# Scores of two attention mixers in clusters of four maps, half of them in borrowed accumulators

## Chip, core and metric

The kernel runs on one core of a Trainium2 chip. The metric is the device time of one execution in microseconds, as the median of several.

## What is computed

Two layers of a decoder trunk with four attention mixers, 256 positions, 1024 channels, four heads per mixer. Cut to what matters here:

```python
xn = rms_norm(x)
h = xn @ w_in                      # columns of the four mixers
# B: two softmax maps per head of 32 channels each
p1 = masked_softmax(q1 @ k1.T * scale); p2 = masked_softmax(q2 @ k2.T * scale)
o_b = rms_norm((p1 - lam * p2) @ v)
# C: with 256 positions, plain causal attention, heads of 64 channels
o_c = masked_softmax(q @ k.T * scale) @ v
# A: stick-breaking attention; D: compressed, selected and window branches
merged = sum(sigmoid(xn @ w_gate[i] + b_gate[i]) * (o_i @ w_branch[i]) for i in 0..3)
x = x + merged @ w_out
x = x + (silu(hn @ w_ffn_gate) * (hn @ w_ffn_up)) @ w_ffn_down    # hn = rms_norm(x)
```

## The kernel before

The five kinds of large products (in, gate, branch, out, ffn and down) stream their weights in chunks of 256 rows by 512 columns (the last input group has 396 columns). A chunk is loaded by SP into `w_raw` (four buffers), copied by ScalarE into `w_hi`, and the remainder is formed by VectorE in `w_lo`; ScalarE and VectorE work two chunks ahead. TensorE then does eight products with `w_hi` and four with `w_lo`, 12 for each chunk (L648). A load of chunk n waits until `w_lo` of chunk n-4 is made.

The attention work lies between the chunks. Each small piece of it is a step with a kind and a name, and the table `PLAN` says in which slot u it stands. All engines walk the slots in the same order. In slot u TensorE does the steps first and then the products of chunk u. ScalarE and VectorE do the steps of a `RANK` below 3, then the split of chunk u+2, then the steps of rank 3 and above, in order of rank. The slots 0 to 23 are the input projection, 24 to 55 the gates, 56 on the branch products.

The steps of this case, per layer:

- `sm` computes causal scores of a pair of maps (`scores`, `causal`, L733). Per map there are two matmuls: the second 128 queries against 256 keys (256 columns), the first 128 against 128 (128 columns). In mixer B a map has 32 channels, so a matmul uses 32 rows of the array; in C, D (and A's `z`) it uses 64. The two maps of a pair lie on different rows, and each writes to its own PSUM bank, S0 or S1 (`maps_of`, `banks_of`). B has four pairs, C two, D four. VectorE then reads both banks with four fused operations, mask and row maximum (L1271); ScalarE takes the four exponentials with sums (L963); VectorE normalises (`p`, L1285 to L1304).
- `pt` transposes probabilities on TensorE into bank TP (L772), and ScalarE copies them out (`ptb`, L1038). `pv` multiplies with V (L788 for B, L797 for the others).
- `qk` transposes queries or keys (L720), `cr` and `kct` are small pieces of D's compressed branch (L851, L862), `ck` and `cv` its compression (L810), `cs` its scores (L872).

The order on an engine is thus written out by hand through `PLAN` and `RANK`. PSUM has eight banks: TP, OB, S0 and S1 for attention, and two pairs `acc` for the results of the large products, which alternate from one result to the next (`bank_pair`). A pair is idle from the time when ScalarE (`proj`) or VectorE (`zg` and the others) has read a result until the next but one result starts.

Of the kernel before, what the change touches and what calls it, by code (L numbers as in the profile page):

```python
# [14 lines left out]
P = 128  # L15
# [34 lines left out]
NCH = len(CHUNKS)  # L50
# [21 lines left out]
def in_cols(g):  # L72
# [40 lines left out]
def maps_of(mixer, n):  # L113
# [11 lines left out]
    "x0": 0, "f0": 0, "m0": 0, "proj": 4, "zg": 4.5, "merge": 0.5, "xadd": 0.5, "act": 3.5, "silu": 4, "hid": 4.5, "split": 5, "rows": 1, "Acum": 5.5,  # L125
    "Dp": 6, "cpv": 6, "sig": 4.5, "Cpv": 3, "cbuild": 1.5, "kct": 4.5, "x": 0.5, "Asp": 6, "Bpv": 4.5, "ck": 1,
    "cv": 1.5, "cs": 3.5, "prep": 0.5, "Csm": 3, "Dpv": 4.5, "lambda": 2.5, "stats": 1.5, "subln": 6, "Bsm": 4,
    "Bpt": 6, "ngate": 1.5, "Cp": 5, "kcprep": 2, "f": 4, "Bp": 5.5,
# [3 lines left out]
def steps():  # L132
# [3 lines left out]
    def put(u, *step):  # L136
        at[u].append(step)
# [11 lines left out]
    for mixer in "ABCD":  # L149
        if mixer != "A":  # L150
            put(PLAN["prep"]["BCD".index(mixer)], "prep", mixer)
        for n in range(PAIRS[mixer]):
            for kind in {"A": ("z", "sp", "cum", "pv"), "B": ("sm", "p")}.get(mixer, ("sm", "p", "pv")):
# [89 lines left out]
TP, OB, S0, S1 = range(4)  # L243


def banks_of(step):
    kind, a = step
    if kind == "pair":
        if a[0] == "o":
            return (TP,) if a[1] == 1 else (OB,)  # L250
        return ((TP, S0, S1, OB)[a[1]],)
    if kind in ("qk", "pt", "kct", "cpt", "cr", "cks"):
        return (TP,)
    if kind in ("z", "cum", "sm", "cs"):
# [50 lines left out]
def trunk_kernel(nc, x, x_t, w_in, w_gate, w_branch, w_out, w_ffn, w_ffn_down,  # L305
                 norm_g, gains, lam, cmp_pe, cmp_w, b_gate, const, masks, out):
    with ExitStack() as ctx:
# [206 lines left out]

        block = ctx.enter_context(nc.Block())
# [70 lines left out]
        def _(pe):  # L586
            def bank_free(l, step):

                for b in banks_of(step):
                    prev = previous(l, BANK_USES[b], step)  # L590
                    if prev:

                        before = ("cum", prev[1][1]) if prev[1][0] == "z" else prev[1]
                        ev = read_dve if reader_of(before) == "dve" else read_act
                        pe.wait_ge(ev.sem, ev.at(prev[0], before))

            def products(l, u):
# [125 lines left out]
            def causal(buf, maps, swap=False):  # L723

                for b in (S0, S1) if swap else ():
                    pe.matmul(att[:, b, :].rearrange("p (s c) -> p s c", c=P)[:, 0:3:2, :], ident16,
                              mask_a.unsqueeze(1).to_broadcast([P, 2, P]), start=True, stop=False, skip_group_check=True)
                first, second = ((0, 2 * P), (P, 2 * P)) if swap else ((0, P), (0, 2 * P))
                areas = ((0, first, 0), (1, second, 2 * P)) if swap else ((1, second, P), (0, first, 0))
                for n, (t, (c0, c1), at) in enumerate(areas):  # L730
                    for i, (r, q, k) in enumerate(maps):
                        still, move = (k, q) if swap else (q, k)
                        mm = pe.matmul(att[:, S0 + i, at:at + c1 - c0], qkt[buf][r, still, t * P:(t + 1) * P],  # L733
                                       qkt[buf][r, move, c0:c1], start=not swap and n == 0, stop=n == 1,
                                       skip_group_check=True)
                return mm

            def scores(l, step):
                kind, a = step
                bank_free(l, step)  # L740
                mixer, n = ("A", a) if kind == "z" else a
                if n == 0:
# [3 lines left out]
                buf, maps = maps_of(mixer, n)  # L746
                mm = causal(buf, maps, swap=mixer == "A")
                mm.then_inc(att_done.now(step), 1)
# [372 lines left out]
        def _(dve):  # L1121
# [36 lines left out]
            def do(l, step):  # L1158
# [103 lines left out]
                elif kind == "sm":  # L1262
# [306 lines left out]
```

## Time and profile before

| | us |
|---|---|
| median of 3 executions | 859.01 (858.69 to 859.31) |
| the profiled execution | 859.28 |
| its span, first to last instruction | 857.5 |
| TensorE busy | 851.2 (99%) |
| VectorE busy | 598.6 (70%) |
| ScalarE busy | 500.4 (58%) |
| GpSimd busy | 267.7 (31%) |
| HBM traffic | 154.45 MB, 180 GB/s |

Durations of single instructions come from the one profiled execution. A row of the timeline gives the start of a group, the time from there to the end of its last instruction, and how many there were; matmul ends are modelled, so the distance from the start of one group to the start of the next is the time that TensorE spent on it. An fp32 matmul of the attention steps is recorded twice (x8 for four matmuls), since it runs in two passes. The two layers show the same pattern, the second some 424 us after the first.

### The profile page before, as it was taken

The page shows a single profiled execution, that of the slowest core. Times are in us where ns is not written, and L with a number is a line of the kernel's source. Part 1 is how long each engine was busy: PE and PEld are TensorE (multiplying, and loading weights), DVE is VectorE, ACT ScalarE, POOL GpSimd, SP SyncE. Part 2 cuts the span into 40 slices and gives each one's busy share as a digit, 9 for nine tenths or more (in the row PEclk, how much of TensorE's full clock was granted, in tenths as well). Part 3 has the DMA queues.
Part 4 walks back from the last instruction along what each step waited for, and adds up shares of the span by engine and source line. Part 5 has one row for each costly group of instructions (what it writes and reads, how often), then busy time and mean ns, then how long its engine had stood idle before and what let it go on. Part 6 is the DMA issues. An engine that isn't in the chain of part 4 may idle for free.

```text
span 857.5 us, 12229 instructions
## 1 busy us (share of the span) xinstructions
PE 851.2 (99%) x4530; PEld 706.0 (82%) x4530; DVE 598.6 (70%) x932; ACT 500.4 (58%) x837; POOL 267.7 (31%) x253
## 2 busy tenths in 40 slices
PE   9999999999999999999999999999999999999998
PEld 6888887787888888888888788878788888888886
DVE  5566868558868888864555668676587698888552
ACT  6785645676457555553457775556654665556431
POOL 0087714003304444420000967230042144444100
PEclk9999999999999999999999999999999999999999
DMA  9756454445656555565565455454445565565652
GB/s 333 248 156 199 153 189 144 149 146 173 195 170 199 192 183 191 179 206 177 172 212 192 136 194 179 167 172 148 143 159 193 169 213 186 184 188 189 201 193 73
DMA packets 68443, 155.24 MB, mean 181 GB/s; under 512 B 5409, under 2 KB 7841, under 8 KB 68129
## 3 DMA queue, kind: packets, MB, share of 16 engines
q1 hardware_dynamic: 68096, 154.20, 55.4%
q8 instruction: 36, 0.59, 0.3%
q10 hardware_dynamic: 288, 0.27, 0.1%
q14 instruction: 23, 0.18, 0.1%
HBM read 153.40 MB, written 1.05 MB: 180 GB/s over the span
## 4 chain that ended last, share of the span: by engine, by line
PE 96%; DMA 1%; DVE 1%; ACT 1%; issue 0%; SPq 0%; ACTq 0%
PE acc L648 60%; PE acc L637 18%; PE acc L642 9%; PE att L733 2%; PE att L797 1%; PE att L772 1%; PE att L695 1%; PE att L720 1%; DMA w_raw<-in_w_in 1%; PE att L788 1%; PE att L756 0%; DVE xs L1204 0%; DVE w_lo L1135 0%; ACT sq_dump L1010 0%; PE att L810 0%
## 5 line engine op out<-in xcount | busy, mean ns | idle before, releaser
L1135 DVE TENSOR_TENSOR w_lo<-w_raw,w_hi 128x1024 fp32r<-128x1024 f32 (+1 forms) x276 | 357.7, 1307 | 121.4 <-ACT w_hi L905 119.3
L905 ACT ACTIVATE w_hi<-w_raw 128x1024 fp32r<-128x1024 f32 (+1 forms) x275 | 286.5, 1051 | 98.0 <-PE acc L648 69.1
L648 PE MATMUL acc<-w_hi,xt 128*128 128x512 f32 (+1 forms) x1024 | 261.8, 397 | 0.2 <-ACT xt L928 0.2
L648 PEld LDWEIGHTS acc<-w_hi,xt 128*128 128x128 f32 x1024 | 185.5, 188 | 38.9 <-issue 2.2
L637 PE MATMUL acc<-xt,w_hi 128*128 128x512 f32 x704 | 176.8, 393 | 0.5 <-DVE xt L1146 0.5
L1486 POOL TENSOR_TENSOR gate_up<-gate_up,rows 128x256 f32<-128x256 f32 x88 | 107.9, 1245 | 140.4 <-DVE gate_up L1209 122.6
L637 PEld LDWEIGHTS acc<-xt,w_hi 128*128 128x128 f32 x704 | 126.7, 189 | 23.6 <-issue 0.9
L648 PE MATMUL acc<-w_lo,xt 128*128 128x512 f32 (+1 forms) x512 | 136.0, 387 | 0.0
L648 PEld LDWEIGHTS acc<-w_lo,xt 128*128 128x128 f32 x512 | 96.0, 188 | 19.6
L642 PEld LDWEIGHTS acc<-xt,w_lo 128*128 128x128 f32 x704 | 96.0, 190 | 6.9
L642 PE MATMUL acc<-xt,w_lo 128*128 128x256 f32 x704 | 98.1, 282 | 0.0
L1393 POOL TENSOR_SCALAR small<-small 128x2 f32<-128x2 f32 (+4 forms) x14 | 9.9, 706 | 228.3 <-ACT sq_dump L1010 129.6
L1493 POOL TENSOR_TENSOR merged<-merged,prod 128x1024 f32<-128x1024 f32 x10 | 32.4, 3240 | 137.5 <-DVE prod L1183 136.6
L987 ACT ACTIVATE gate_up<-acc 128x256 f32<-128x256 f32 x88 | 29.0, 382 | 69.5 <-PE acc L642 68.8
L963 ACT ACTIVATE eb<-eb,small 128x128 f32<-128x128 f32 x80 | 35.5, 444 | 49.3 <-DVE small L1271 49.3
L1209 DVE TENSOR_TENSOR gate_up<-acc,gate_up 128x256 f32<-128x256 f32 x88 | 33.2, 418 | 29.4 <-ACT gate_up L987 29.4
L648 PE MATMUL acc<-w_hi,ht_hi 128*128 128x512 f32 x176 | 47.8, 390 | 0.0
L648 PE MATMUL acc<-w_hi,ht_lo 128*128 128x512 f32 x176 | 47.6, 389 | 0.0
L648 PE MATMUL acc<-w_lo,ht_hi 128*128 128x512 f32 x176 | 47.5, 389 | 0.0
L1221 DVE TENSOR_TENSOR ht_lo<-hid,ht_hi 128x256 fp32r<-128x256 f32 x44 | 39.9, 908 | 0.0
L648 PEld LDWEIGHTS acc<-w_hi,ht_lo 128*128 128x128 f32 x176 | 33.0, 188 | 6.9
L648 PEld LDWEIGHTS acc<-w_lo,ht_hi 128*128 128x128 f32 x176 | 33.0, 188 | 6.9
(172 smaller groups left out, 815.4 us busy)
## 6 DMA issues: line engine op xcount, KB each, us to landing
w_raw<-in_w_ffn SPq DMA_DIRECT2D x88, 512.0 KB, 4.0
w_raw<-in_w_gate SPq DMA_DIRECT2D x64, 512.0 KB, 3.6
w_raw<-in_w_ffn_down SPq DMA_DIRECT2D x44, 512.0 KB, 4.1
w_raw<-in_w_in SPq DMA_DIRECT2D x39, 512.0 KB, 5.0
w_raw<-in_w_branch SPq DMA_DIRECT2D x16, 512.0 KB, 4.0
w_raw<-in_w_out SPq DMA_DIRECT2D x16, 512.0 KB, 3.5
bg<-in_b_gate SPq DMA_DIRECT2D x8, 512.0 KB, 5.2
w_raw<-in_w_in SPq DMA_DIRECT2D x8, 396.0 KB, 3.4
```

Source lines behind the costliest of these rows:

```text
L637: pe.matmul(acc[bank0 + i][:, :], wh4[:, k, i * FC:(i + 1) * FC], xt[:, 4 * b + k, :, :].rearrange("p i t -> p (i t)"), start=first and k ...
L642: mm = pe.matmul(acc[bank0 + i][:, 0:SEQ], wl4[:, k, i * FC:(i + 1) * FC], xt_hi[:, 4 * b + k, :], start=False, stop=last and k == 3)
L648: return pe.matmul(acc[bank0 + t][:, 0:N], x_part[:, k0 + k, t * P:(t + 1) * P], w_part[:, k, 0:N], start=first, stop=last)
L733: mm = pe.matmul(att[:, S0 + i, at:at + c1 - c0], qkt[buf][r, still, t * P:(t + 1) * P], qkt[buf][r, move, c0:c1], start=not swap and n == ...
L905: act.activation(w_hi[:, n % WR, :, 0:N], w_raw[:, n % RAW, :, 0:N], copy).then_inc(s_hi, 1)
L963: ins = act.activation(eb[:, e, cols], eb[:, e, cols], ACT.Exp, scale=-1.0, bias=nbias[r][:, j:j + 1], accum_out=sums[r][:, j:j + 1])
L987: ins = act.activation(gate_up[:, a % 2, i, :], acc[bank_pair(l, step) + i][:, 0:SEQ], copy)
L1135: dve.tensor_tensor(w_lo[:, n % WR, :, 0:N], w_raw[:, n % RAW, :, 0:N], w_hi[:, n % WR, :, 0:N].bitcast(F32), ALU.subtract).then_inc(s_lo, 1)
L1209: ins = dve.tensor_tensor(gate_up[:, a % 2, i, :], acc[bank_pair(l, step) + i][:, SEQ:], gate_up[:, a % 2, i, :], ALU.add)
L1221: dve.tensor_tensor(ht_lo[:, a, :], hid[:, a % 2, :], ht_hi[:, a, :].bitcast(F32), ALU.subtract).then_inc(ht_lo_done.now(step), 1)
L1486: ins = pool.tensor_tensor(gate_up[:, a % 2, i, :], gate_up[:, a % 2, i, :], rows[:, :], ALU.mult)
L1493: pool.tensor_tensor(merged[:, :, cols], merged[:, :, cols], prod[:, :, half_], ALU.add).then_inc(pool_done.now(step), 1)
```

## The change

`sm` steps of B and C stand two by two in one slot: `Bsm` goes from (21, 24, 27, 28) to (21, 21, 27, 27), `Csm` from (35, 36) to (35, 35). The second step of such a cluster (`second`) has no matmul code of its own; the first step issues both. Its scores go to the pair of accumulators that the chunk products running at that time don't use: that of the next result (`IDLE_OF`, bank name IDLE). `bank_free` waits for it until the result before has been read and until the earlier use of this kind has been read; `products` makes the first chunk of the next result wait until VectorE has read the scores (three clusters a layer). `score_matmuls` orders the four maps of B together (all 256-column matmuls, then all 128-column ones) and those of C pair after pair. D and A keep pairs. VectorE reads from `score_bank`.

Also moved by `PLAN`: B's `pt` of its first map from slot 23 to 24, B's `pv` of its third from 31 to 33, `p` of C's first pair from 36 to 35, and the four sigmoids from (48, 52, 56, 56) to (49, 53, 57, 57). In the branch for `put`, all `sm` steps of a mixer are entered ahead of its `p` steps. `RANK` is only laid out anew.

```diff
-    "sig": (48, 52, 56, 56), "o": (22, 44, 44, 58), "subln": 36, "prep": (13, 18, 25), "ngate": 25, "Aq": 6,
+    "sig": (49, 53, 57, 57), "o": (22, 44, 44, 58), "subln": 36, "prep": (13, 18, 25), "ngate": 25, "Aq": 6,
-    "Bsm": (21, 24, 27, 28), "Bp": (21, 24, 27, 29), "Bpt": (23, 27, 29, 32), "Bpv": (27, 29, 31, 35), "Bo": 36,
-    "Cq": 25, "Ck": 33, "Csm": (35, 36), "Cp": (36, 40), "Cpt": (39, 40, 42, 42), "Cpv": (43, 43), "Dc": 27,
+    "Bsm": (21, 21, 27, 27), "Bp": (21, 24, 27, 29), "Bpt": (24, 27, 29, 32), "Bpv": (27, 29, 33, 35), "Bo": 36,
+    "Cq": 25, "Ck": 33, "Csm": (35, 35), "Cp": (35, 40), "Cpt": (39, 40, 42, 42), "Cpv": (43, 43), "Dc": 27,
...
+def second(step):
+    kind, a = step
+    return kind == "sm" and a[1] % 2 == 1 and PLAN[a[0] + "sm"][a[1]] == PLAN[a[0] + "sm"][a[1] - 1]
...
+IDLE_USES = [s for s in ORDER if second(s)]
+IDLE_OF = {s: RESULTS[result_at(SLOT[s]) + 1] for s in IDLE_USES}
...
+        def score_bank(l, step, i):
+
+            return acc[bank_pair(l, IDLE_OF[step]) + i] if second(step) else att[:, S0 + i, :]
...
+                    if b == IDLE:
+                        n = RESULTS.index(IDLE_OF[step]) - 2
+                        before = RESULTS[n]
+                        ev = proj_out if before[0] == "proj" else dve_acc
+                        pe.wait_ge(ev.sem, ev.at(l, before))
+                        if IDLE_USES.index(step):
+                            before = IDLE_USES[IDLE_USES.index(step) - 1]
+                            pe.wait_ge(read_dve.sem, read_dve.at(l, before))
+                        continue
...
+                for s in IDLE_USES if first else ():
+                    if IDLE_OF[s] == step:
+                        pe.wait_ge(read_dve.sem, read_dve.at(l, s))
...
+            def score_matmuls(l, todo, swap=False):
+
+                for t in (0, 1) if swap else (1, 0):
+                    for step, n, buf, (r, q, k) in todo:
+                        still, move, c0, c1, at = (k, q, t * P, 2 * P, 2 * P * t) if swap else (q, k, 0, (t + 1) * P, t * P)
+                        mm = pe.matmul(score_bank(l, step, n)[:, at:at + c1 - c0], qkt[buf][r, still, t * P:(t + 1) * P],
+                                       qkt[buf][r, move, c0:c1], start=not swap and t == 1, stop=t == (1 if swap else 0),
+                                       skip_group_check=True)
+                        if t == (1 if swap else 0) and n == 1:
+                            mm.then_inc(att_done.now(step), 1)
...
+                if mixer == "B":
+                    score_matmuls(l, sum(todo, []))
+                else:
+                    for maps in todo:
+                        score_matmuls(l, maps, swap=kind == "z")
...
-                            ins = dve.tensor_tensor_reduce(out=eb[:, e, cols], in0=att[:, S0 + i, cols],
+                            ins = dve.tensor_tensor_reduce(out=eb[:, e, cols], in0=score_bank(l, step, i)[:, cols],
```

How the order moves, at three places. First TensorE, slots 21 to 24 of the first layer, mixer B's first two score steps (`qkt_75` holds B's queries and keys); before:

```order
L733 MATMUL att<-qkt_75 128x256 x2
L733 MATMUL att<-qkt_75 128x128 x2
L648 MATMUL acc<-w_hi,xt 128x396 x8
L648 MATMUL acc<-w_lo,xt 128x396 x4
L797 MATMUL att<-ptb,proj 64x256 x2
L797 MATMUL att<-ptb,proj 64x128 x2
L648 MATMUL acc<-w_hi,xt 128x396 x8
L648 MATMUL acc<-w_lo,xt 128x396 x4
L772 MATMUL att<-cst,eb 128x128 x3
L648 MATMUL acc<-w_hi,xt 128x396 x8
L648 MATMUL acc<-w_lo,xt 128x396 x4
L733 MATMUL att<-qkt_75 128x256 x2
```

and after the change, where L767 are the score matmuls, L687 the chunk products, L821 the transposes and L846 the products with V (from the second row of the step on; the first is `att` with 256 columns as before):

```order
L767 MATMUL acc<-qkt_75 128x256 x2
L767 MATMUL att<-qkt_75 128x128 x2
L767 MATMUL acc<-qkt_75 128x128 x2
L687 MATMUL acc<-w_hi,xt 128x396 x8
L687 MATMUL acc<-w_lo,xt 128x396 x4
L846 MATMUL att<-ptb,proj 64x256 x2
L846 MATMUL att<-ptb,proj 64x128 x2
L687 MATMUL acc<-w_hi,xt 128x396 x8
L687 MATMUL acc<-w_lo,xt 128x396 x4
L687 MATMUL acc<-w_hi,xt 128x396 x8
L687 MATMUL acc<-w_lo,xt 128x396 x4
L821 MATMUL att<-cst,eb 128x128 x3
```

The second step's four matmuls, which stood in slot 24, stand among those of the first and write to `acc`; the transpose has moved from slot 23 to 24.

Second TensorE, slots 35 and 36, mixer C's two score steps (`qkt_74` holds C's); before:

```order
L733 MATMUL att<-qkt_74 128x256 x2
L733 MATMUL att<-qkt_74 128x128 x2
L851 MATMUL att<-vcs,cst 128x64
L788 MATMUL att<-proj,ptb 128x64 x3
L648 MATMUL acc<-w_hi,xt 128x512 x8
L648 MATMUL acc<-w_lo,xt 128x512 x4
L733 MATMUL att<-qkt_74 128x256 x2
L733 MATMUL att<-qkt_74 128x128 x2
L862 MATMUL att<-cst,kcs 128x16
```

and after:

```order
L767 MATMUL att<-qkt_74 128x256 x2
L767 MATMUL att<-qkt_74 128x128 x2
L767 MATMUL acc<-qkt_74 128x256 x2
L767 MATMUL acc<-qkt_74 128x128 x2
L900 MATMUL att<-vcs,cst 128x64
L837 MATMUL att<-proj,ptb 128x64 x3
L687 MATMUL acc<-w_hi,xt 128x512 x8
L687 MATMUL acc<-w_lo,xt 128x512 x4
L911 MATMUL att<-cst,kcs 128x16
```

C's second pair follows the first as a whole; slot 36 keeps only the small transpose.

Third ScalarE, slots 21 to 24, with the exponentials of B's first two pairs (`eb`), the chunk copies (`w_hi`) and the reading of transposed probabilities (`ptb`); before:

```order
L963 ACTIVATE eb,small<-eb,small 128x128
L963 ACTIVATE eb,small<-eb,small 128x256
L905 ACTIVATE w_hi<-w_raw 128x1024
L930 ACTIVATE ot_hi<-att 128x512
L905 ACTIVATE w_hi<-w_raw 128x1024
L1038 ACTIVATE ptb<-att 128x384
L905 ACTIVATE w_hi<-w_raw 128x1024
L977 ACTIVATE proj<-acc,small 128x396 x2
L963 ACTIVATE eb,small<-eb,small 128x128
L963 ACTIVATE eb,small<-eb,small 128x256
L963 ACTIVATE eb,small<-eb,small 128x128
```

and after:

```order
L1012 ACTIVATE eb,small<-eb,small 128x128
L1012 ACTIVATE eb,small<-eb,small 128x256
L1012 ACTIVATE eb,small<-eb,small 128x128
L1012 ACTIVATE eb,small<-eb,small 128x256
L1012 ACTIVATE eb,small<-eb,small 128x128
L1012 ACTIVATE eb,small<-eb,small 128x256
L954 ACTIVATE w_hi<-w_raw 128x1024
L979 ACTIVATE ot_hi<-att 128x512
L954 ACTIVATE w_hi<-w_raw 128x1024 x2
L1026 ACTIVATE proj<-acc,small 128x396 x2
L1087 ACTIVATE ptb<-att 128x384
```

The second pair's four exponentials stand ahead of the copy for chunk 24, no longer behind the projection's read, and the read of the transposed probabilities stands behind that.

## Rows read from the trace of the kernel before

**Rows 1.** The page's busy times, and busy times in one stretch (columns as the line says).
```profile
PE 851.2 (99%) x4530; PEld 706.0 (82%) x4530; DVE 598.6 (70%) x932; ACT 500.4 (58%) x837; POOL 267.7 (31%) x253
...
core 0: us, PE busy (x) PEld busy (x) DVE busy (x) ACT busy (x) POOL busy (x), PEclk, DMA share, GB/s
72.42:97.06 24.64, 24.64 (x146) 20.58 (x145) 17.71 (x49) 17.63 (x47) 16.45 (x23) 1.00 0.55 178
```
**Rows 2.** The chain that ended last, by engine.
```profile
PE 96%; DMA 1%; DVE 1%; ACT 1%; issue 0%; SPq 0%; ACTq 0%
```
**Rows 3.** What TensorE waited for: total us, times, longest.
```profile
PE att L772 <- ACT ptb L1038: 1.2, 2, 0.6
```
**Rows 4.** Timeline of TensorE, slots 23 and 24: start us, length us, engine, line, form.
```profile
78.00 0.89 PE L648 MATMUL acc<-w_lo,xt 128*128 128x396 f32 x4
78.72 0.49 PE L772 MATMUL att<-cst,eb 128*128 128x128 f32 x3
...
80.49 0.89 PE L648 MATMUL acc<-w_lo,xt 128*128 128x396 f32 x4
81.31 0.92 PE L733 MATMUL att<-qkt 32*128 32x256 f32 x8
82.16 1.19 PE L648 MATMUL acc<-w_hi,xt 128*128 128x512 f32 x4
```
**Rows 5.** Timeline of TensorE, slots 26 to 28.
```profile
90.02 1.07 PE L648 MATMUL acc<-w_lo,xt 128*128 128x512 f32 x4
90.92 0.60 PE L720 MATMUL att<-cst,kcdup 128*128 128x128 f32 x4
...
92.31 0.88 PE L788 MATMUL att<-proj,ptb 128*128 128x64 f32 x6
...
95.21 1.07 PE L648 MATMUL acc<-w_lo,xt 128*128 128x512 f32 x4
...
97.06 1.19 PE L648 MATMUL acc<-w_hi,xt 128*128 128x512 f32 x4
```
**Rows 6.** Timeline of instants 72.44 and 73.07, inside one score step.
```profile
72.42 0.19 PEld L733 LDWEIGHTS att<-qkt 32*128 32x128 f32 x2 [0.27 <-issue]
72.42 0.48 PE L733 MATMUL att<-qkt 32*128 32x256 f32 x2
...
72.74 0.60 PE L733 MATMUL att<-qkt 32*128 32x256 f32 x6
72.96 0.19 PEld L733 LDWEIGHTS att<-qkt 32*128 32x128 f32 x2
```
**Rows 7.** Timeline of TensorE, slot 36.
```profile
124.54 1.08 PE L648 MATMUL acc<-w_lo,xt 128*128 128x512 f32 x4
...
126.41 0.23 PE L862 MATMUL att<-cst,kcs 16*128 16x16 f32 x1
126.57 0.74 PE L648 MATMUL acc<-w_hi,xt 128*128 128x512 f32 x2
```
**Rows 8.** Timeline of TensorE: compression products, compressed scores.
```profile
106.44 1.10 PE L810 MATMUL att<-cw,cblk 128*32 128x64 f32 x64
...
135.48 1.09 PE L872 MATMUL att<-kct,qkt 64*128 64x16 f32 x16
```
**Rows 9.** Timeline of VectorE, slots 21, 27 and 35.
```profile
73.69 0.28 DVE L1271 CUSTOM_DVE_ANT_0 eb<-att,cst 128x128 f32<-128x128 f32 x1
...
89.62 3.79 DVE L1135 TENSOR_TENSOR w_lo<-w_raw,w_hi 128x1024 fp32r<-128x1024 f32 x3
93.32 0.28 DVE L1271 CUSTOM_DVE_ANT_0 eb<-att,cst 128x128 f32<-128x128 f32 x1
...
121.81 0.29 DVE L1271 CUSTOM_DVE_ANT_0 eb<-att,cst 128x128 f32<-128x128 f32 x1 [0.81 <-PE att L733]
```
**Rows 10.** Timeline of ScalarE, slots 21 to 24.
```profile
74.91 0.40 ACT L963 ACTIVATE eb<-eb,small 128x128 f32<-128x128 f32 x1 [2.50 <-DVE small L1271]
...
76.69 1.04 ACT L905 ACTIVATE w_hi<-w_raw 128x1024 fp32r<-128x1024 f32 x1
...
81.42 1.07 ACT L977 ACTIVATE proj<-acc,small 128x396 f32<-128x396 f32 x2 [0.73 <-PE acc L648]
```

More of the change, by code:

```diff
@@ L124 @@
 RANK = {
[L125 to L128, printed above, removed]
+    "x0": 0, "f0": 0, "m0": 0, "proj": 4, "zg": 4.5, "merge": 0.5, "xadd": 0.5, "act": 3.5, "silu": 4,
+    "hid": 4.5, "split": 5, "rows": 1, "Acum": 5.5, "Dp": 6, "cpv": 6, "sig": 4.5, "Cpv": 3, "cbuild": 1.5,
+    "kct": 4.5, "x": 0.5, "Asp": 6, "Bpv": 4.5, "ck": 1, "cv": 1.5, "cs": 3.5, "prep": 0.5, "Csm": 3,
+    "Dpv": 4.5, "lambda": 2.5, "stats": 1.5, "subln": 6, "Bsm": 4, "Bpt": 6, "ngate": 1.5, "Cp": 5, "kcprep": 2,
+    "f": 4, "Bp": 5.5,
 }
@@ L151, in steps @@
             put(PLAN["prep"]["BCD".index(mixer)], "prep", mixer)
+        for n in range(PAIRS[mixer] if mixer != "A" else 0):
+            put(PLAN[mixer + "sm"][n], "sm", (mixer, n))
         for n in range(PAIRS[mixer]):
-            for kind in {"A": ("z", "sp", "cum", "pv"), "B": ("sm", "p")}.get(mixer, ("sm", "p", "pv")):
+            for kind in {"A": ("z", "sp", "cum", "pv"), "B": ("p",)}.get(mixer, ("p", "pv")):
                 put(PLAN[mixer + kind][n], kind, n if mixer == "A" and kind != "pv" else (mixer, n))
@@ L239, in now, with result_at @@
         return self.sem
-TP, OB, S0, S1 = range(4)
+TP, OB, S0, S1, IDLE = range(5)
+def second(step):
+    kind, a = step
+    return kind == "sm" and a[1] % 2 == 1 and PLAN[a[0] + "sm"][a[1]] == PLAN[a[0] + "sm"][a[1] - 1]
+SLOT = {s: u for u in range(NCH + 1) for s in STEPS[u]}
+def result_at(u):
+    kind, a, b = CHUNKS[u]
+    return RESULTS.index({"in": ("proj", a), "gate": ("zg", a)}[kind])
+IDLE_USES = [s for s in ORDER if second(s)]
+IDLE_OF = {s: RESULTS[result_at(SLOT[s]) + 1] for s in IDLE_USES}
 def banks_of(step):
@@ L253, in banks_of @@
         return (TP,)
+    if second(step):
+        return (IDLE,)
     if kind in ("z", "cum", "sm", "cs"):
@@ L721, in qk @@
                 mm.then_inc(att_done.now(step), 1)
[L723 to L734, printed above, removed]
+            def score_matmuls(l, todo, swap=False):
[4 more added lines that the diff above has]
+                                       qkt[buf][r, move, c0:c1], start=not swap and t == 1, stop=t == (1 if swap else 0),
                                        skip_group_check=True)
-                return mm
+                        if t == (1 if swap else 0) and n == 1:
+                            mm.then_inc(att_done.now(step), 1)
             def scores(l, step):
                 kind, a = step
-                bank_free(l, step)
+                if second(step):
+                    return
                 mixer, n = ("A", a) if kind == "z" else a
+                group = [step] + [s for s in IDLE_USES if kind == "sm" and s[1] == (mixer, n + 1)]
+                for s in group:
+                    bank_free(l, s)
                 if n == 0:
@@ L745, in scores @@
                         pe.wait_ge(s_mask16, 1)
-                buf, maps = maps_of(mixer, n)
-                mm = causal(buf, maps, swap=mixer == "A")
-                mm.then_inc(att_done.now(step), 1)
+                todo = []
+                for s in group:
+                    buf, maps = maps_of(mixer, s[1] if kind == "z" else s[1][1])
+                    todo.append([(s, i, buf, m) for i, m in enumerate(maps)])
+                if kind == "z":
+                    for b in (S0, S1):
+                        pe.matmul(att[:, b, :].rearrange("p (s c) -> p s c", c=P)[:, 0:3:2, :], ident16,
+                                  mask_a.unsqueeze(1).to_broadcast([P, 2, P]), start=True, stop=False, skip_group_check=True)
+                if mixer == "B":
[3 more added lines that the diff above has]
+                        score_matmuls(l, maps, swap=kind == "z")
             def cumulate(l, step):
```

## The prediction

> **What bounds the kernel now.** I read the page's first parts, then the chain of waits, then TensorE's waits, then TensorE's timeline around the score steps, and only last the two engines that read the scores. TensorE is busy for 851.2 us of 857.5 at the full granted clock [rows 1]. The chain that ended last is TensorE for 96% [rows 2], and what TensorE waited for on ScalarE in the attention steps is 1.2 us in all [rows 3]. So between the layer's ends nothing but TensorE's own work sets the time. Each microsecond taken from it comes off the end, as long as VectorE and ScalarE, busy for 17.7 and 17.6 us of the 24.6 us around mixer B's steps [rows 1], stay ahead.
>
> **What a score step costs.** The ordinary step from a chunk's last products to what follows takes 0.72 us in the 396-column chunks (78.00 to 78.72) and 0.90 us in the 512-column ones (90.02 to 90.92) [rows 4, 5]. With B's second step between, 80.49 to 82.16 are 1.67 us, so the step costs 0.95. With B's fourth, 95.21 to 97.06 are 1.85 us, 0.95 again [rows 4, 5]. What is in it: the four matmuls are recorded as eight passes. Two weight loads and two passes start together at 72.42, on two row tiles [rows 6]. The later rows start at 72.74 and 72.96, so a round of 256 columns takes 0.22 us, and one of 128 columns half of that, 0.11 [rows 6]. Two rounds of each are 0.66 us of streaming. The other 0.29 us of the 0.95 is entering and leaving the row-tiled shape.
>
> **The change, part by part.**
>
> *Mixer B, four clusters in two layers.* Each removes a step of 0.95 us (slots 24 and 28) and puts its four matmuls on the two row tiles that stood idle in the step of slot 21 or 27. B uses 32 rows per matmul, so all four fit at once, each into its own bank. No row of before has four row tiles. From below, the added matmuls cost nothing, if they run wholly beside the first pair as the first two do beside each other. From above, they cost a second streaming, 0.66 us, if the pairs follow one another. Nearest are the rows of two kinds in which the array runs in pieces. The compression products keep four column tiles going: 64 recorded matmuls take 1.10 us, 17 ns each [rows 8]. And the compressed scores (16 passes on two row tiles, several of one tile ahead of the other in program order) take 1.09 us, about the 0.11 us that a load takes for each of eight rounds, so the second tile doesn't stand behind the first one's queue [rows 8]. I take the lower end with 0.03 us for the issue of two more matmuls (2 x 17 ns). That gives 4 x (0.95 - 0.03) = 3.7 us.
>
> *Mixer C, one cluster per layer.* C uses 64 rows, so its second pair needs the same two row tiles and follows the first: the clusters only save a change of shape. Removed in slot 36: 124.54 to 126.41 is 1.87 us [rows 7], against 0.90 plus 0.10 for the entry into the 16-row transpose (L862) that now has to be paid by itself (the entry is what 0.95 holds over the 0.85 from 81.31 to 82.16 [rows 4]). That is 0.87. Added in slot 35: 0.66. Net 0.21 per layer, 0.4 us in all. From above it could be 0.3 per layer (all of the 0.29), from below nothing.
>
> *Moved steps.* B's first transpose of probabilities goes from slot 23 to 24 and its third product with V from slot 31 to 33, unchanged in number. They cost TensorE what they did. At most the product escapes the 0.10 us of a change of shape behind the compression; I count nothing. The sigmoids stand one slot later on ScalarE, which has no part in the chain worth a line [rows 2] and is hidden by the chunk products. If that cover went, the product of sigmoid and branch on VectorE would be late first, then the accumulator of the next branch product. No DMA is added, and none moves in the program; but a load waits for w_lo four chunks before, so what is late on ScalarE delays SP's issues as well.
>
> *Added waits.* In slot 21 the second pair needs the accumulators that ScalarE has emptied of projection 4; that work is two slots old. The first products of the next result wait for VectorE's reading of the second pair. That is the dangerous one, because the whole weight stream is queued behind it. In slot 21 three chunks lie between, in slots 27 and 35 only one. Slot 27: TensorE finishes the cluster 0.95 us before its 92.31, at 91.4, and would start chunk 28 at 96.11 - 0.95 = 95.2 (96.11 being 95.21 + 0.90) [rows 5]. VectorE needs 1.22 us for one pair (from 73.69 to 74.91, when ScalarE's first exponential takes over) [rows 9, 10], 2.4 us for both. If it begins at once, it ends at 93.8 to 94.0, with over 1 us to spare; it also waits for the transpose of slot 27, which TensorE does 0.7 us after the cluster. In before it came to this step only at 93.32, behind three w_lo passes of 3.79 us [rows 9]. These stood behind preparation D on ScalarE, and that behind the 1.8 us of B's second exponentials (a step runs from 74.91 to 76.69 [rows 10]). These exponentials now come earlier, in slot 21, so that VectorE should be free about 1.8 us sooner, at 91.5. Slot 35: VectorE starts at 121.81 [rows 9] and is through with both pairs at 124.3; chunk 36 begins near 126.4 (126.57 [rows 7] plus 0.66 for the longer cluster less the 0.87 removed).
>
> *ScalarE in slot 21.* It now does two steps of exponentials, 76.69 to 78.5, before w_hi of chunk 24, which is ready at 79.5 instead of 77.7 (76.69 + 1.04 [rows 10]). TensorE needs it at 82.16 - 0.95 = 81.2. Its lead is two chunks, and it sat idle for 0.73 us before the projection's read at 81.42 [rows 10], so it has caught up before slot 25. Cost nothing; that lead is the cover.
>
> **Sum.** 3.7 + 0.4 = 4.1 us. The profiled execution took 859.28 us, so it would take 855.2. The median shown is 859.01, 0.27 us less, so I forecast 854.9.
>
> **A rule against it.** The rows show two row tiles at no loss: both passes of a round start at 72.42 [rows 6]. The Trainium skill, "TensorE: Matmul & The Clock Gate", section "Measured speedup vs the span model", gives four row tiles of 32 rows 3.07 times the speed of one at 512 columns. By that rule a round would last 4 / 3.07 = 1.3 times as long, the streaming grow from 0.66 to 0.86 us, and the sum be an estimated 3.3 us instead of 4.1. The nearest row for four tiles, the compression, has rounds of 1.10 / 16 = 0.069 us for 64 columns, where a quarter of 0.22 is 0.055 [rows 6, 8]; that is 25% over, or 16% if 0.08 us of it are change of shape.
>
> **The rivals.**
> 1. *Four streams hinder one another.* For it: the compression's rounds, 16% or more longer than one stream's. Against it: a score round is long enough (0.11 to 0.22 us) to hide the issue of four matmuls with their loads at 17 ns each. Price 0.10 to 0.17 us a cluster, 0.4 to 0.7 us: 855.5. Of the rule above: 855.7.
> 2. *The pairs follow one another.* Each B cluster then costs another 0.66 us and saves only 0.29. The sum is 4 x 0.29 + 0.4 = 1.6 us: 857.4. Against it: nothing serial in [rows 6, 8].
> 3. *The lent accumulator comes back late.* If VectorE reaches slot 27's step no sooner than in before, it ends at 93.32 + 2 x 1.22 = 95.8, and chunk 28 waits 0.6 us per layer, 1.2 us in all: 856.1. The Trainium skill's "TensorEngine Tiling (Array Packing)", section "PSUM Bottleneck", warns of just this: tiling speeds up TensorE but not the emptying of its results. The trace agrees so far as 2.4 us of reading stand against 0.95 us of matmuls.
> 4. *A pace other than TensorE's.* Loads or the split of the weights give the saved time back before the layer's end: within 0.2% of before, 859. Against it: TensorE waited in the list for no chunk but at the seams [rows 3].
> 5. *The four run one by one* (slower). If a cluster of four is worked off tile by tile, it streams 4 x 0.66 = 2.64 us and takes 2.93 with the change of shape, against two steps of 0.95: 1.03 us more, four times, less 0.4 for C, is +3.7: 862.7. It turns slower once a cluster takes more than 2.0 us. Against it: the same hardware does two tiles in parallel.
>
> **How the numbers follow.** Forecast (854.3 to 855.2) 0.62; rival 1 0.12; rival 2 0.08; rival 3 0.09; rival 4 0.06; rival 5 0.03. About 0.2% (1.7 us) is what a measurement of this kernel can tell from no change, so faster means below 857.3. Rivals 1 and 3 lie there wholly and rival 2 with some of its chance: faster 0.90, same 0.07, slower 0.03. The best case is 3.8 + 0.6 for C + 0.1 = 4.5 us, 854.5, and the subtractions above are good to 0.01 us each, some 0.3 us over both layers: low end 854.1. Leaving out rivals 2, 4 and 5 (0.17), the range ends at 857.0.
>
> **What would show it.** In the profile after: score rows of 16 recorded matmuls on 32 rows with a next start 0.85 to 0.9 us later, and four weight loads starting within some 20 ns; about 1.5 us in C's cluster; TensorE's busy time down by 4 us, and no new wait of its accumulate products on VectorE's score reading. A cluster of 1.5 us would be rival 2, one of 2.9 rival 5. A new idle time before chunk 28 or 36 would be rival 3. Wrong altogether would be a lower busy time with the same span.

## The result, and the profile after

The changed kernel takes 854.22 us (median, 853.99 to 854.79) against 859.05 for the one before: a ratio of 0.9945, 95% interval 0.9934 to 0.9957, or 4.8 us less (3.7 to 5.7). Forecast were 854.9, a range of 854.1 to 857.0, and 0.90 for faster by over 0.2%. The same kernel measured again, beside the last experiments, took 854.55 us against 858.87, 4.3 us less, so the gain is known as 4.3 to 4.8 us. The profiled execution took 854.36 us, its span is 852.5. The page's lines that answer to [rows 1, 2]:

```profile
span 852.5 us, 12229 instructions
...
PE 846.1 (99%) x4530; PEld 703.4 (83%) x4530; DVE 597.2 (70%) x932; ACT 500.1 (59%) x837; POOL 259.4 (30%) x253
...
PE 97%; DVE 1%; ACT 1%; DMA 1%; issue 0%; SPq 0%; ACTq 0%
```

TensorE's busy time fell by 5.1 us, the span by 5.0. VectorE's and ScalarE's (598.6 to 597.2, 500.4 to 500.1) stayed: the work is the same, TensorE alone does its part in less time. What TensorE waited for (total us, times, longest) answers to [rows 3]:

```profile
PE att L821 <- ACT ptb L1087: 1.2, 2, 0.6
```

There is no wait for the lent accumulators, and the one at the transposes is what it was. The other rows of the list lie at the start and at the feed-forward's seam. TensorE's timeline in slots 21 and 22 (start us, length us, engine, line, form) shows the cluster whose second half writes to `acc`:

```profile
72.21 0.49 PE L767 MATMUL att<-qkt 32*128 32x256 f32 x2
72.22 0.48 PE L767 MATMUL acc<-qkt 32*128 32x256 f32 x2
72.53 0.38 PE L767 MATMUL att<-qkt 32*128 32x256 f32 x2
72.55 0.38 PE L767 MATMUL acc<-qkt 32*128 32x256 f32 x2
72.75 0.28 PE L767 MATMUL att<-qkt 32*128 32x128 f32 x2
72.76 0.28 PE L767 MATMUL acc<-qkt 32*128 32x128 f32 x2
72.86 0.28 PE L767 MATMUL att<-qkt 32*128 32x128 f32 x2
72.87 0.28 PE L767 MATMUL acc<-qkt 32*128 32x128 f32 x2
73.08 1.72 PE L687 MATMUL acc<-w_hi,xt 128*128 128x396 f32 x8
```

Sixteen recorded matmuls on 32 rows, in rounds of four that start within 0.01 to 0.02 us of each other, and the next start 73.08 - 72.21 = 0.87 us after the first: a pair took 0.85 (81.31 to 82.16 in [rows 4]). At the instant 72.24 two and two weight loads are under way:

```profile
72.21 0.19 PEld L767 LDWEIGHTS att<-qkt 32*128 32x128 f32 x2 [0.27 <-issue]
...
72.22 0.19 PEld L767 LDWEIGHTS acc<-qkt 32*128 32x128 f32 x2
```

Mixer C, slots 35 and 36:

```profile
120.09 0.43 PE L900 MATMUL att<-vcs,cst 128*128 128x64 f32 x2
...
122.93 1.07 PE L687 MATMUL acc<-w_lo,xt 128*128 128x512 f32 x4
123.93 0.23 PE L911 MATMUL att<-cst,kcs 16*128 16x16 f32 x1
124.09 2.14 PE L687 MATMUL acc<-w_hi,xt 128*128 128x512 f32 x8
```

and the cluster's beginning, one row of a view a little earlier:

```profile
118.58 0.92 PE L767 MATMUL att<-qkt 64*128 64x256 f32 x8
```

C's pair in slot 35 before:

```profile
120.84 0.92 PE L733 MATMUL att<-qkt 64*128 64x256 f32 x8
121.69 0.43 PE L851 MATMUL att<-vcs,cst 128*128 128x64 f32 x2
```

C's cluster takes 120.09 - 118.58 = 1.51 us where the pair took 0.85; that is the 0.66 us of the second streaming. Slot 36 takes 123.93 - 122.93 = 1.00 us to the start of the small transpose instead of 1.87 [rows 7]: 0.87 gone.

VectorE, slot 27, answers to [rows 9]:

```profile
88.08 2.36 DVE L1184 TENSOR_TENSOR w_lo<-w_raw,w_hi 128x1024 fp32r<-128x1024 f32 x2 [0.15 <-ACT w_hi L954]
91.21 0.29 DVE L1320 CUSTOM_DVE_ANT_0 eb<-att,cst 128x128 f32<-128x128 f32 x1 [0.77 <-PE acc L767]
...
92.50 0.29 DVE L1320 CUSTOM_DVE_ANT_0 eb<-acc,cst 128x128 f32<-128x128 f32 x1
...
93.27 0.42 DVE L1320 CUSTOM_DVE_ANT_0 eb<-acc,cst 128x256 f32<-128x256 f32 x1
```

It stood ready 0.77 us before the cluster was done, where before it came late at 93.32. It read the second pair from 92.50 (after the transpose for which it has to wait) to 93.7. TensorE started chunk 28 at 94.92, so VectorE was through 1.2 us before. In slot 35 it was through with both pairs at 121.9, and chunk 36 started at 124.09. ScalarE, slots 21 to 24, answers to [rows 10]:

```profile
74.69 0.40 ACT L1012 ACTIVATE eb<-eb,small 128x128 f32<-128x128 f32 x1 [2.50 <-DVE small L1320]
...
78.22 1.04 ACT L954 ACTIVATE w_hi<-w_raw 128x1024 fp32r<-128x1024 f32 x1
...
81.54 1.04 ACT L1026 ACTIVATE proj<-acc,small 128x396 f32<-128x396 f32 x2
82.49 0.47 ACT L1087 ACTIVATE ptb<-att 128x384 f32<-128x384 f32 x1
82.86 0.90 ACT L1100 ACTIVATE kdup<-proj 128x128 f32<-128x128 f32 x4
```

Two steps of exponentials, 74.69 to 78.22, and then no idle time until 89.0, well behind the projection's read. By then it is 3.0 us ahead of where it was: preparation D (`kdup`) starts at 82.86, in the trace of before at 85.82.

### The profile page after: what moved, and what is told of

Same layout as the page of the kernel before. It is cut to its first block, busy times and chain, and to the rows that moved or that the text cites. A ratio compares the mean times of both kernels' runs of the same rounds, so it can differ in the third digit from the quotient of the medians.

```text
span 852.5 us, 12229 instructions
## 1 busy us (share of the span) xinstructions
PE 846.1 (99%) x4530; PEld 703.4 (83%) x4530; DVE 597.2 (70%) x932; ACT 500.1 (59%) x837; POOL 259.4 (30%) x253
## 4 chain that ended last, share of the span: by engine, by line
PE 97%; DVE 1%; ACT 1%; DMA 1%; issue 0%; SPq 0%; ACTq 0%
PE acc L687 60%; PE acc L676 18%; PE acc L681 9%; PE att L767 2%; PE att L846 1%; PE att L821 1%; PE att L734 1%; PE att L759 1%; PE att L837 1%; DMA w_raw<-in_w_in 1%; PE att L805 0%; DVE xs L1253 0%; DVE w_lo L1184 0%; ACT sq_dump L1059 0%; PE att L859 0%
## 5 line engine op out<-in xcount | busy, mean ns | idle before, releaser
L687 PE MATMUL acc<-w_hi,xt 128*128 128x512 f32 (+1 forms) x1024 | 261.1, 397 | 0.4 <-ACT w_hi L948 0.2
L687 PEld LDWEIGHTS acc<-w_hi,xt 128*128 128x128 f32 x1024 | 185.5, 188 | 39.1 <-issue 2.2
L687 PE MATMUL acc<-w_lo,xt 128*128 128x512 f32 (+1 forms) x512 | 136.0, 388 | 0.0
L687 PEld LDWEIGHTS acc<-w_lo,xt 128*128 128x128 f32 x512 | 96.0, 188 | 19.5
L1442 POOL TENSOR_SCALAR small<-small 128x2 f32<-128x2 f32 (+4 forms) x14 | 7.6, 542 | 226.0 <-ACT sq_dump L1059 129.4
L687 PE MATMUL acc<-w_hi,ht_hi 128*128 128x512 f32 x176 | 47.8, 391 | 0.0
L687 PE MATMUL acc<-w_hi,ht_lo 128*128 128x512 f32 x176 | 47.6, 389 | 0.0
L687 PE MATMUL acc<-w_lo,ht_hi 128*128 128x512 f32 x176 | 47.6, 389 | 0.0
L687 PEld LDWEIGHTS acc<-w_hi,ht_lo 128*128 128x128 f32 x176 | 33.0, 188 | 6.9
L687 PEld LDWEIGHTS acc<-w_lo,ht_hi 128*128 128x128 f32 x176 | 33.0, 188 | 6.9
```

The lines of the kernel that those rows point to most:

```text
L687: return pe.matmul(acc[bank0 + t][:, 0:N], x_part[:, k0 + k, t * P:(t + 1) * P], w_part[:, k, 0:N], start=first, stop=last)
```

## The experiments

Times are medians. The kernel before took 858.91 us beside the first four experiments, 858.97 beside four others (the moved places alone, the triple reading, D's cluster, and D's cluster between two transposes) and 858.87 beside the last three (the old places, the changed kernel again, and B's output transposed first). Diffs are against the changed kernel where nothing else is said.

**C's cluster alone.**

```diff
-    "Bsm": (21, 21, 27, 27), "Bp": (21, 24, 27, 29), "Bpt": (24, 27, 29, 32), "Bpv": (27, 29, 33, 35), "Bo": 36,
+    "Bsm": (21, 24, 27, 28), "Bp": (21, 24, 27, 29), "Bpt": (23, 27, 29, 32), "Bpv": (27, 29, 31, 35), "Bo": 36,
```

> The changed kernel with B's score steps, its first transpose and its third product with V back in their old slots; C's cluster stays, and so do the moved sigmoids. If most of the gain comes from four row tiles at once (theory), C's cluster alone gives 0.2 us a layer (0.87 removed, 0.66 added), 0.4 us in all: 858.6, which a measurement can hardly tell from before. If the gain comes from fewer changes of shape and fewer steps between chunks (rival), C's cluster gives the same as one of B's, about 0.8 us, 1.6 in two layers: 857.4.

Measured: 858.58 us, ratio 0.9996 (0.9987 to 1.0006). C's cluster is worth 0.3 us, if anything, as the theory has it; 1.6 us are excluded.

**B's clusters alone.**

```diff
-    "Cq": 25, "Ck": 33, "Csm": (35, 35), "Cp": (35, 40), "Cpt": (39, 40, 42, 42), "Cpv": (43, 43), "Dc": 27,
+    "Cq": 25, "Ck": 33, "Csm": (35, 36), "Cp": (36, 40), "Cpt": (39, 40, 42, 42), "Cpv": (43, 43), "Dc": 27,
```

> The changed kernel with C's second pair back in slot 36. Theory: B's four clusters carry all but 0.4 us of the 4.8 measured: 854.6 to 854.8, VectorE and ScalarE as in the changed kernel up to slot 34. Rival (all clusters worth the same, about 0.8 us): 855.8.

Measured: 854.87 us, ratio 0.9952 (0.9938 to 0.9967). With the run before, the two parts add up: 4.0 and 0.3 us against 4.3 to 4.8 for both together. The time is 0.07 us above the range that the theory gave. A cluster of B is worth 1.0 us, one of C 0.2.

**B's four maps on two row tiles.** The scores of B's odd pairs are here those of the even ones.

```diff
     if mixer == "B":
-        rows = [slice(64 * (n % 2) + 32 * i, 64 * (n % 2) + 32 * i + 32) for i in range(2)]
+        rows = [slice(32 * i, 32 * i + 32) for i in range(2)]
```

> The changed kernel, but B's odd pairs take their queries and keys from the rows of the even pairs, so that the four maps of a cluster share two row tiles; the scores of the odd pairs are then those of the even ones. Instructions, banks, waits and places are unchanged. Theory: the streaming of the second pair (two rounds of 0.22 us and two of 0.11) is no longer beside the first: the cluster's next start is 1.53 us after its own instead of 0.87, four times 0.66: 856.8. Rival (the tiles of the second pair add nothing, the gain is the saved change of shape and the saved step): 854.2, as the changed kernel.

Measured: 856.92 us, ratio 0.9977 (0.9967 to 0.9986), 2.4 to 2.7 us more than the changed kernel. Its timeline of TensorE, slot 21:

```profile
72.15 0.70 PE L767 MATMUL att<-qkt 32*128 32x256 f32 x4
72.69 0.60 PE L767 MATMUL acc<-qkt 32*128 32x256 f32 x4
73.12 0.39 PE L767 MATMUL att<-qkt 32*128 32x128 f32 x4
73.34 0.39 PE L767 MATMUL acc<-qkt 32*128 32x128 f32 x4
73.66 1.55 PE L687 MATMUL acc<-w_hi,xt 128*128 128x396 f32 x7
```

The same sixteen passes now go two by two, and the next start is 1.51 us after the first instead of 0.87. This is the direct test of the parallel tiles: everything but the rows is unchanged, and the second pair costs 0.64 us. It also says how the gain of a B cluster splits: some 0.64 us from four tiles at once, the rest from the saved step. That rest is 0.4 us a cluster: (858.58 - 856.92) / 4, against the run with C's cluster alone.

**Pair after pair in the program.**

```diff
-                if mixer == "B":
-                    score_matmuls(l, sum(todo, []))
-                else:
-                    for maps in todo:
-                        score_matmuls(l, maps, swap=kind == "z")
+                for maps in todo:
+                    score_matmuls(l, maps, swap=kind == "z")
```

> The changed kernel, but a B cluster issues the first pair's four matmuls and then the second pair's, instead of all four of 256 columns and then all four of 128. If each row tile has its own queue, the cluster stays at 0.87 us, 854.2. If matmuls start in the order of the program, the second pair begins when the first pair's last round does, two rounds of 256 columns and one of 128 later (0.55 us), and the cluster takes 1.4 us: 856.3. I hold the first for likelier, since the compressed scores of before kept two tiles going although several passes of one tile stand ahead of the other's in the program.

Measured: 854.52 us, in a single execution. Its timeline of TensorE, slot 21:

```profile
72.31 0.48 PE L767 MATMUL att<-qkt 32*128 32x256 f32 x2
72.33 0.48 PE L767 MATMUL acc<-qkt 32*128 32x256 f32 x2
```

The second pair starts 0.02 us after the first, though four matmuls (eight passes) stand ahead of it in the program, and the chunk follows 0.87 us after the cluster's start (73.18). So the order within a cluster doesn't matter at this size, and the regrouping by `sum(todo, [])` brings nothing of its own.

**The moved places without the clusters** (against the kernel before).

```diff
-    "sig": (48, 52, 56, 56), "o": (22, 44, 44, 58), "subln": 36, "prep": (13, 18, 25), "ngate": 25, "Aq": 6,
+    "sig": (49, 53, 57, 57), "o": (22, 44, 44, 58), "subln": 36, "prep": (13, 18, 25), "ngate": 25, "Aq": 6,
-    "Bsm": (21, 24, 27, 28), "Bp": (21, 24, 27, 29), "Bpt": (23, 27, 29, 32), "Bpv": (27, 29, 31, 35), "Bo": 36,
+    "Bsm": (21, 24, 27, 28), "Bp": (21, 24, 27, 29), "Bpt": (24, 27, 29, 32), "Bpv": (27, 29, 33, 35), "Bo": 36,
```

> The kernel before with only the moved places: B's first transpose in slot 24 beside its second score step, its third product with V in slot 33, the sigmoids one slot later. No cluster. Theory on the part of the gain that I had not counted: a chunk that follows another chunk starts 0.08 to 0.13 us faster than one that follows a step, so slots 23 and 31 gain some 0.1 us each, 31 less what slot 33 pays; 0.1 to 0.2 us a layer, 858.6 to 858.8. Rival (the moved places are worth the 0.4 us or more that the forecast lacked, by a wait that they take away): 858.4 or less, with a wait gone from TensorE's list.

Measured: 862.04 us, ratio 1.0035 (1.0022 to 1.0049). Both expectations missed: by themselves the places cost 3.1 us. TensorE's waits, and ScalarE's timeline in slot 24:

```profile
PE att L720 <- ACT ptb L1038: 2.7, 2, 1.5
```

```profile
83.65 0.41 ACT L963 ACTIVATE eb<-eb,small 128x128 f32<-128x128 f32 x1 [1.88 <-DVE small L1271]
...
85.42 0.47 ACT L1038 ACTIVATE ptb<-att 128x384 f32<-128x384 f32 x1
```

With the score step in slot 24 as well, ScalarE does B's second exponentials (83.65 to 85.42) before it empties the transpose bank at 85.42; slot 25's transposes of C's queries need that bank, and wait 1.2 us behind a chunk whose work was done, 1.5 in the second layer. Counted from start to start, the distance from the chunk's last products to these transposes grows from 0.91 us to 2.26 and 2.54, which is 3.0 us of the 3.1. The cluster had taken these exponentials to slot 21. The places are good only together with it.

**The old places with the clusters.**

```diff
-    "sig": (49, 53, 57, 57), "o": (22, 44, 44, 58), "subln": 36, "prep": (13, 18, 25), "ngate": 25, "Aq": 6,
+    "sig": (48, 52, 56, 56), "o": (22, 44, 44, 58), "subln": 36, "prep": (13, 18, 25), "ngate": 25, "Aq": 6,
-    "Bsm": (21, 21, 27, 27), "Bp": (21, 24, 27, 29), "Bpt": (24, 27, 29, 32), "Bpv": (27, 29, 33, 35), "Bo": 36,
+    "Bsm": (21, 21, 27, 27), "Bp": (21, 24, 27, 29), "Bpt": (23, 27, 29, 32), "Bpv": (27, 29, 31, 35), "Bo": 36,
```

> The changed kernel with its clusters, but B's first transpose back in slot 23, its third product with V in 31 and the sigmoids in their old slots. Theory: the moved places are worth only what one chunk gains that no longer follows a step (0.07 us in slot 23), 0.1 to 0.3 us in all: 854.3 to 854.5; the loss of 3 us that these places brought without the clusters has to do with B's second exponentials standing in slot 24, which the cluster has moved to slot 21. Rival: the places are worth some us by themselves, since two steps of exponentials stand in one slot and the transposed map in slot 23 is read late; TensorE would then wait for ScalarE at the transposes of slot 25 or at slot 23, and the time be 855 or more.

Measured: 854.34 us, ratio 0.9946 (0.9929 to 0.9962). Beside it the changed kernel once more:

> The changed kernel itself, beside the two others of this call: 854.2 (853.9 to 854.8).

Measured: 854.55 us, ratio 0.9947 (0.9933 to 0.9962). The two don't differ by more than their spread, and neither has a wait at slot 23 or 25. With the clusters, the moved places are worth nothing that can be measured. The timeline says why: with the old places the chunk of slot 23 takes 1.52 us behind its transpose and that of slot 24 1.85 behind a chunk; in the changed kernel they take 1.44 behind a chunk and 1.95 behind the transpose.

**VectorE reads the fourth pair three times.**

```diff
-                    for i in range(2):
+                    rounds = 3 if a == ("B", 3) else 1
+                    for again in range(rounds):
+                        for i in range(2):
...
+                        if again < rounds - 1:
+                            settled(ins)
```

> The changed kernel, but VectorE reads the scores of B's fourth pair three times instead of once, each time after the one before, 2.4 to 2.6 us more in slot 27 (two more rounds of 1.2 us). In the changed kernel VectorE is through 1.2 us before chunk 28 starts. Theory (the lent accumulators have a margin of 1.2 us, and beyond it each microsecond is TensorE's): chunk 28 waits 1.2 to 1.4 us, 2.4 to 2.8 us in two layers, 856.6 to 857.0. Rival (nothing in the attention steps is so tight, the weight stream absorbs it): 854.2 to 854.5. More than 857.2 would mean that the delay hits other steps as well.

Measured: 857.30 us, ratio 0.9981 (0.9972 to 0.9990). TensorE's timeline:

```profile
94.00 1.07 PE L687 MATMUL acc<-w_lo,xt 128*128 128x512 f32 x4
96.30 2.09 PE L687 MATMUL acc<-w_hi,xt 128*128 128x512 f32 x8 [1.23 <-DVE small L1322]
98.23 1.09 PE L687 MATMUL acc<-w_lo,xt 128*128 128x512 f32 x4
```

Chunk 28 starts at 96.30, 2.30 us after the last products of chunk 27 instead of 0.91: 1.4 us a layer for 2.5 us of added reading. So the margin at slot 27 is 1.1 us; the timeline's 1.2 also holds the 0.15 us from VectorE's last row (96.15) to TensorE's start. Beyond the margin the rest of the added reading is TensorE's wait, as far as one length of delay can show it. The time lies 0.3 us above the theory's range, and above the 857.2 that I had called a sign of other steps being hit. None is: TensorE's list has no other new wait. What the theory lacked is that the chunk behind the wait is slower. Its eight products with `w_hi` take 98.23 - 96.30 = 1.93 us, in the second layer 1.91, where they take 1.81 without the wait. With that it is 1.5 us a layer, 3.0 in all, of the 3.1 measured. Rival 3 of the prediction is a true mechanism with 1.1 us left before it acts.

**D's first two pairs in a cluster.**

```diff
-    "cpt": 41, "cpv": 45, "Dq": 34, "Dk": 38, "Dsm": (40, 42, 46, 52), "Dp": (41, 42, 47, 52),
-    "Dpt": (43, 45, 47, 50, 51, 53, 55, 56), "Dpv": (46, 55, 55, 57),
+    "cpt": 41, "cpv": 45, "Dq": 34, "Dk": 38, "Dsm": (42, 42, 46, 52), "Dp": (42, 42, 47, 52),
+    "Dpt": (44, 45, 47, 50, 51, 53, 55, 56), "Dpv": (46, 55, 55, 57),
```

> The changed kernel with D's first two pairs (64 rows, as C's) in a cluster in slot 42, the first moved there from 40 with its normalisation, and D's first transpose from slot 43 to 44. Theory: as with C, the second pair's streaming of 0.66 us is paid in full; gone are 0.86 us of the step and the 0.16 us that the transpose before it took longer for its change to the row shape; 0.3 to 0.4 us a layer: 853.4 to 853.6. Rival (ScalarE, which has two steps of exponentials, 3.6 us, in one slot, is late with a transposed map or a chunk): a new wait of TensorE in slots 43 to 46 and 854.2 or more.

Measured: 855.15 us, ratio 0.9956 (0.9939 to 0.9972), 0.6 to 0.9 us more than the changed kernel. The wait that is new:

```profile
PE att L734 <- ACT ptb L1087: 1.2, 2, 0.6
```

```profile
153.43 0.49 PE L821 MATMUL att<-cst,eb 128*128 128x128 f32 x3
154.50 0.66 PE L734 MATMUL att<-cst,osb 128*128 128x128 f32 x4 [0.58 <-ACT ptb L1087]
```

A new wait has come, but at none of the places that I had named: D's first transpose now stands in slot 44 directly ahead of the transposes of B's output (L734), and both use the one transpose bank, which ScalarE has to empty between them. The list has 0.58 us of waiting for it in each layer, but the second group starts 1.07 us after the first, where other work starts 0.25 us after such transposes (93.02 to 93.28 in the trace of before): 0.82 us a layer. The theory's gain is there, 0.37 us in the first layer (1.03 gone in slots 40 and 41, 0.66 added in slot 42), and the new wait more than eats it.

**D's cluster between two transposes.** It takes two transposes of C apart that waited on each other in the same way in every kernel so far (L772 in [rows 3]). The diff is against the run before.

```diff
-    "Cq": 25, "Ck": 33, "Csm": (35, 35), "Cp": (35, 40), "Cpt": (39, 40, 42, 42), "Cpv": (43, 43), "Dc": 27,
+    "Cq": 25, "Ck": 33, "Csm": (35, 35), "Cp": (35, 40), "Cpt": (39, 40, 42, 42), "Cpv": (44, 44), "Dc": 27,
...
 def rank(step):
+    if step == ("pt", ("C", 3)):
+        return 4.2
```

> As the kernel with D's cluster, but the cluster stands between the two transposes of slot 42, whose second waits 0.58 us for ScalarE to empty the transpose bank, and C's products with V go from slot 43 to 44. Theory: the cluster covers that wait, 0.58 us a layer, so 1.2 us less than the kernel with the cluster behind them: 852.3. Rival (ScalarE now reads the second transpose only after both steps of exponentials, so the products with V in slot 44 wait for it): TensorE's list shows a wait at the products with V, and the time stays above 853.4.

Measured: 853.36 us, ratio 0.9935 (0.9920 to 0.9949), 1.8 us less than the run before where 1.2 was expected. The 852.3 was missed too, since it was reckoned from D's cluster without its new wait. The wait at C's transposes is gone, the one at L734's step still there (1.2 us in two layers). As the rival has it the time stays near 853.4, but its wait at the products with V didn't come. The timeline of the first layer has the extra: slot 42 gives 0.82 us for a wait listed with 0.58, and some 0.1 more comes from slots 43 and 44 with C's products moved. The run changes both places at once; how much each is worth by itself was not run.

**B's output transposed ahead of C's products with V** (again against the run before).

```diff
 def rank(step):
     if step == ("pt", ("C", 3)):
         return 4.2
+    if step == ("pair", ("o", 1)):
+        return 2.5
```

> The kernel with D's cluster between the two transposes of slot 42, and in slot 44 the transposes of B's output ahead of C's products with V instead of behind D's transpose. Theory: the wait of 0.58 us a layer before those transposes goes, since the transpose bank was emptied in slot 42 and D's transpose finds it emptied again behind 1.45 us of products: 1.2 us less than the 853.4 of that kernel, 852.2, and no wait of TensorE in the attention steps. Rival (ScalarE's copy and VectorE's remainder of B's output, 1.3 us, take longer than the products): the wait moves to D's transpose, 852.5 to 853.4.

Measured: 852.05 us (851.79 to 852.36), ratio 0.9918 (0.9904 to 0.9933). All that TensorE still waited for, and the slots' timeline:

```profile
PE att L871 <- DVE warm L1206: 1.2, 1, 1.2
PE acc L691 <- ACT xt L981: 0.6, 1, 0.6
PE acc L680 <- DVE xt L1199: 0.5, 2, 0.3
```

```profile
151.18 0.60 PE L738 MATMUL att<-cst,osb 128*128 128x128 f32 x4
151.71 1.52 PE L850 MATMUL att<-ptb,proj 128*64 128x256 f32 x16
153.19 0.55 PE L825 MATMUL att<-cst,eb 128*128 128x128 f32 x3
153.50 2.09 PE L691 MATMUL acc<-w_hi,xt 128*128 128x512 f32 x8
```

No wait is left in the attention steps (the three rows are the start and the feed-forward's seam), and both parts of the expectation held. This version beats both kernels: 6.8 us less than the one before, 2.5 less than the changed one beside it (854.55).

## Why the prediction was right, point by point

- *What bounds.* TensorE's own work, and nothing else. It held: 5.1 us less busy time, 5.0 less span.
- *Mixer B, 0.95 a step less 0.03 of issue.* The cluster's 0.87 us against 0.85 is the issue cost, 0.02. The tiles run in parallel, as the experiment on two row tiles shows by taking it away. But the step removed was worth more than 0.95. This is the term that I had sized too small: I measured the step from the last products of one chunk to the first of the next and overlooked that the next chunk itself is slower behind a step. Slot 28 before (the products with `w_hi` start at 97.06 [rows 5]):

```profile
99.01 1.08 PE L648 MATMUL acc<-w_lo,xt 128*128 128x512 f32 x4
```

and after:

```profile
94.92 1.98 PE L687 MATMUL acc<-w_hi,xt 128*128 128x512 f32 x8
96.73 1.08 PE L687 MATMUL acc<-w_lo,xt 128*128 128x512 f32 x4
```

The eight products with `w_hi` take 99.01 - 97.06 = 1.95 us behind the score step and 96.73 - 94.92 = 1.81 behind another chunk. So slot 28 gave 0.95 + 0.14 = 1.09 us. In slot 24 a step stays, the transpose that left slot 23, and slot 23's chunk got 0.08 (1.52 to 1.44 us). In the second layer that transpose also came 0.1 us late before, right behind VectorE's normalisation; no list has this as a wait. Why the first chunk behind a step is slower stays open, but the step itself isn't needed. It is so behind a transpose, which uses the full array (1.93 and 1.95 us), behind the 16-row transpose (1.98), and behind nothing but a wait of 1.23 us, as the triple reading shows (1.93). So it isn't the change of shape alone. That the other 0.29 us of the step are entering and leaving the row-tiled shape, as the prediction has it, no run separates either; the runs show 0.66 us of streaming (0.64 in the run on two row tiles) and a rest.
- *Mixer C, 0.21 a layer.* 0.87 removed and 0.66 added, both to 0.01 us in the timeline, and 0.3 us for both layers in the run.
- *The sum.* Slot 21's chunk starts before at

```profile
73.27 1.72 PE L648 MATMUL acc<-w_hi,xt 128*128 128x396 f32 x8
```

From there to the chunk of slot 36, before and after: 126.57 - 73.27 = 53.30 us and 124.09 - 73.08 = 51.01. That is 2.29 us in the first layer where 2.05 was forecast. The second layer gives 2.4. The rest of the 5.0 us of the profiles lies mostly (0.2) before slot 21 (72.42 and 72.21): the same chunks of the input group start up to 0.6 us apart in the profiles of this study (71.79 to 72.42 for slot 21's step), whatever the kernel. 4.7 us by the timeline, 4.3 to 4.8 by the medians, 4.1 forecast.
- *The range.* The mechanism was right and the size near its edge. 4.7 us is more than the 4.5 that the prediction calls its best case, and 854.22 lies just below the 854.3 to 855.2 that had 0.62; the second median, 854.55, lies inside. The low end of 854.1 also doesn't follow from its own terms: 859.01 - 4.5 - 0.3 is 854.2. So it took some luck that the range held; what it had room for was 0.3 us of reading error, not a slower chunk behind a step.
- *Moved steps, nothing.* Right with the clusters, as the run with the old places shows, but my reason was thin. I had asked what hides them, not in which slots they are free: the transpose in slot 24 is free only because the exponentials have left it. Without that it costs 1.5 us a layer.
- *Added waits, nothing.* Right, with the margin that I had given (over 1 us at slot 27, measured 1.1). VectorE came to slot 27 sooner than forecast: not at 91.5 but at 90.4, where it waited for TensorE. I had counted only the 1.8 us of exponentials that leave slot 24; the 1.56 us for which ScalarE stood idle ahead of them (82.49 to 84.05 in the trace of before) went too.
- *ScalarE in slot 21.* w_hi of chunk 24 forecast at 79.5, less 0.2 for the start; it was ready at 78.22 + 1.04 = 79.3. Nothing waited. It had not caught up before slot 25, though, as I had said: it shows no idle time before 89.0, when TensorE is in slot 26.
- *The rule against it.* The Trainium skill, "TensorE: Matmul & The Clock Gate", section "Measured speedup vs the span model", has 3.07 for four row tiles at 512 columns. The cluster's 0.87 us against 0.85 for two tiles leaves at most 0.02 us over 0.66 of streaming, 3%, at 256 and 128 columns of fp32; there the trace doesn't agree with the rule's figure. At 512 columns no run here has four row tiles. Its span model in the same section (a few ns for each further tile) is near the 0.01 us between the starts in the rows. Rivals 1, 2 and 5 fell with it.
- *Rival 4* (another pace) fell: the span followed the busy time.

## What to carry to other kernels

Where TensorE is busy all the time, small matmuls that use 32 rows should go four at once, each into its own bank; an accumulator that is idle for one chunk will do, if its reader is through before the next result starts, and that margin should be read off the timeline. Price a step by two distances: from the work before it to the work after it, and the length of that next work, which was slower here behind any step. Before moving a step that uses a shared bank, look at what the engine that empties the bank does first in that slot; two uses of one bank back to back cost here 0.58 us of waiting and 0.8 us from start to start each time, and putting other work between them was worth more than a cluster of C or D (0.2 and 0.4 us), though less than one of B (1.0). A listed wait cost more here than its figure: 0.82 us for 0.58, and 1.5 us for 1.23 before chunk 28.

## What the runs showed of the hardware

- Four row tiles of fp32 passes, 256 and 128 columns, ran with no loss that counts: 0.87 us for sixteen passes, 0.85 for eight.
- The second pair started 0.02 us after the first even with eight passes of other tiles ahead of it in the program (72.31 and 72.33), and the cluster took the same 0.87 us.
- A chunk's first eight products (512 columns) took 1.81 us behind other products of its kind (1.83 to 1.85 behind the 396-column ones), 1.92 to 2.04 behind a small step of another kind, and 1.91 to 1.93 behind a mere wait of 1.2 us.
- Two groups of transposes through one bank that ScalarE empties between them started 1.07 us apart, instead of 0.25; the list of waits shows 0.58 of it.
